# A streaming-encoder layer on one core: the opening stage loads, squares, scales and turns x's first tiles two to three slots later

## The reference

```python
h = rmsnorm(x, ln_gain)                       # x is 2048 tokens x 2048
proj = h @ w_in                               # queries, keys, values, gates, conv inputs
o_a = swa_sink_attention(q_a, k_a, v_a, ...)  # sliding window, sinks, relative bias
o_c = short_gated_conv(b_c, c_c, x_c, conv_w)
mem_h = rmsnorm(mem, mem_ln_gain)             # mem is 256 tokens x 2048
o_m = memory_cross_attention(q_m, mem_h, w_mem_kv, ...)
x = x + concat(silu(g_a) * o_a, silu(g_c) * o_c, silu(g_m) * o_m) @ w_out
```

## Time and profile before

| | us |
|---|---|
| median of three runs | 2578.4 (2577.44 to 2578.68) |
| the profiled execution | 2577.82 |
| its span | 2575.9 |
| PE busy in the span | 2561.8 (99%) |
| DVE, ACT, POOL busy | 1774.2, 1265.2, 1712.6 |
| the opening stage on PE | from 9.46 to 71.61 |

### The profile page before, as it was taken

How to read it: one execution, slowest core, us unless ns; L and a number is a source line. 1 busy time by engine, 2 the same in 40 slices (tenths; PEclk the granted TensorE clock), 3 DMA queues, 4 the chain that set the end, 5 groups by cost and what they waited for, 6 DMA issues and landing times.

```text
span 2575.9 us, 33864 instructions
## 1 busy us (share of the span) xinstructions
PE 2561.8 (99%) x11846; PEld 2112.8 (82%) x11846; DVE 1774.2 (69%) x2257; ACT 1265.2 (49%) x2629; POOL 1712.6 (66%) x1207
## 2 busy tenths in 40 slices
PE   8999999999999999999999999999999999999999
PEld 6888888888888888888888888888888888888887
DVE  6467675575746757467576767887578686887767
ACT  6454554545545555454554554544444454454443
POOL 6587667885678856787545665757567475665747
PEclk9999999999999999999999999999999999999999
DMA  7677767777667776676767443355645444334534
GB/s 252 202 253 226 245 182 242 255 232 235 192 235 262 232 236 190 231 256 226 234 191 240 146 154 101 98 163 188 197 158 169 148 139 137 96 111 139 188 111 150
DMA packets 324205, 492.26 MB, mean 191 GB/s; under 512 B 18038, under 2 KB 134852, under 8 KB 317892
## 3 DMA queue, kind: packets, MB, share of 16 engines
q1 hardware_dynamic: 209076, 296.63, 37.2%
q10 hardware_dynamic: 114960, 193.48, 21.9%
HBM read 367.61 MB, written 97.25 MB: 180 GB/s over the span
## 4 chain that ended last, share of the span: by engine, by line
PE 95%; DVE 2%; DMA 1%; ACT 1%; issue 0%; POOL 0%; SPq 0%; ACTq 0%; DVEq 0%
PE acc L1897 14%; PE acc L1899 14%; PE acc L1898 14%; PE acc L2002 7%; PE acc L2004 7%; PE acc L2006 7%; PE acc L1971 2%; PE ps_o L2006 2%; PE ps_s L2002 2%; PE ps_s L2004 2%; PE ps_s L2006 2%; PE ps_z L2002 2%; PE ps_t L2002 2%; PE ps_z L2006 2%; PE ps_o L2002 2%; PE ps_o L2004 2%
## 5 line engine op out<-in xcount | busy, mean ns | idle before, releaser
L792 POOL TENSOR_TENSOR w_both<-raw,w_both 128x512 fp32r<-128x512 f32 x889 | 1240.0, 1406 | 789.3 <-ACT w_both L918 785.2
L918 ACT ACTIVATE w_both<-raw 128x512 fp32r<-128x512 f32 x896 | 558.1, 630 | 968.5 <-PE acc L1899 335.1
L1897 PE MATMUL acc<-h_hi,w_both 128*128 128x512 f32 x768 | 311.0, 405 | 0.0
L1897 PE MATMUL acc<-w_both,h_hi 128*128 128x512 f32 x768 | 301.5, 393 | 0.0
L1899 PE MATMUL acc<-h_hi,w_both 128*128 128x512 f32 x768 | 299.6, 390 | 0.0
L1898 PE MATMUL acc<-h_lo,w_both 128*128 128x512 f32 x768 | 299.4, 390 | 0.0
L1899 PE MATMUL acc<-w_both,h_lo 128*128 128x512 f32 x768 | 299.1, 389 | 0.0
L1898 PE MATMUL acc<-w_both,h_hi 128*128 128x512 f32 x768 | 299.0, 389 | 0.0
L1763 DVE TENSOR_TENSOR a_lo<-s_sum,a_hi 128x512 fp32r<-128x512 f32 x192 | 201.7, 1085 | 87.7 <-ACT a_hi L1214 86.0
L2002 PE MATMUL acc<-w_both,a_hi 128*128 128x512 f32 x448 | 174.6, 390 | 1.6 <-DVE a_lo L1763 1.6
L2006 PE MATMUL acc<-w_both,a_lo 128*128 128x512 f32 x448 | 174.3, 389 | 0.0
(11 more groups left out here) (288 smaller groups left out, 5632.3 us busy)
## 6 DMA issues: line engine op xcount, KB each, us to landing
raw<-in_w_in SPq DMA_DIRECT2D x256, 512.0 KB, 4.6
raw<-w_sums SPq DMA_DIRECT2D x128, 512.0 KB, 3.7
w_sums<-stage ACTq DMA_DIRECT2D x32, 1024.0 KB, 5.1
probs_t<-blocks_t SPq DMA_DIRECT2D x384, 64.0 KB, 2.5
raw<-in_w_out SPq DMA_DIRECT2D x48, 512.0 KB, 3.6
stage<-in_w_in ACTq DMA_DIRECT2D x32, 512.0 KB, 5.8
h_rows<-early ACTq DMA_DIRECT2D x16, 1024.0 KB, 7.4
half_rows<-ungated ACTq DMA_DIRECT2D x16, 1024.0 KB, 8.2
```

Source lines behind the costliest of these rows:

```text
L792: nc.gpsimd.tensor_tensor(w_lo[:, at, :], raw[:, slot_mod, HALF * half:HALF * half + HALF], w_hi[:, at, :].bitcast(F32), ALU.subtract).the ...
L918: nc.scalar.activation(w_hi[:, 2 * (slot_mod % 2) + half, :], raw[:, slot_mod, HALF * half:HALF * half + HALF], ACT.Copy).then_inc(hi_read ...
L1897: nc.tensor.matmul(dst, st[0], mv[0], start=first, stop=False)
```

## The change

The change touches only the opening stage. Nothing is computed differently.

- The loads of x0 to x3 are started in slots 0, 2, 3 and 5 (`FIRST_X_LOAD_AT`); before, x0's came ahead of slot 0 and the others in slots 0, 1 and 2.
- ACT's squares: mem0 and mem1 in slots 0 and 1, x0 to x3 in slots 3, 5, 6 and 8 (`FIRST_SQUARE_AT`, now from slot to tile). Before: mem0, x0, x1, x2, mem1, x3 in slots 0 to 5. The mean on DVE follows in the same slot, the root on POOL one slot later, now always behind that slot's `low`.
- DVE's scales of x0 to x3 are in slots 5, 7, 8 and 9 (`FIRST_SCALE_AT`); before, two in slots 3 and 4, and the last after the loop.
- The 16 turns follow slots 10 to 15, with 2, 3, 2, 3, 3, 3 of them; before, slots 7 to 15 with 1, 2, 2, 2, 2, 1, 2, 2, 2.
- The semaphore counts are by tile, since the tiles now go in order.

```diff
-FIRST_TURNS = [[]] * 7 + [[0], [1, 2], [3, 4], [5, 6], [7, 8], [9], [10, 11], [12, 13], [14, 15]]
+FIRST_TURNS = [[]] * 10 + [[0, 1], [2, 3, 4], [5, 6], [7, 8, 9], [10, 11, 12], [13, 14, 15]]
-FIRST_SQUARE_AT = (0, 2, 3, 4, 1, 5)
+FIRST_SQUARE_AT = {0: 0, 1: 1, 3: 2, 5: 3, 6: 4, 8: 5}
-FIRST_X_LOAD_AT = {0: 1, 1: 2, 2: 3}
+FIRST_X_LOAD_AT = {0: 0, 2: 1, 3: 2, 5: 3}
-FIRST_SCALE_AT = {3: (1,), 4: (2, 3)}
+FIRST_SCALE_AT = {5: 2, 7: 3, 8: 4, 9: 5}
...
 POOL:
             for s in range(MEM_SLOTS):
-                if s == LAST_RSQRT:
-                    first_root(s - 1)
                 low((s + 2) % 4, s + 2)
-                if 0 < s < LAST_RSQRT:
-                    first_root(s - 1)
+                if s - 1 in FIRST_SQUARE_AT:
+                    first_root(FIRST_SQUARE_AT[s - 1])
...
 DVE, after slot 7:
-            first_low(0)
+            first_scale(FIRST_SCALE_AT[SB_SLOTS])
             mem_keys = stage[:, 2:4, :].rearrange("p m c -> p (m c)")
-            key_means(mem_keys, xt[:, 0:1024], M_HEAD, 1, mem_raw, FIRST_TURNS[SB_SLOTS])
-            before_scale = FIRST_TURNS[SB_SLOTS + 1][-1] + 1
-            for k in FIRST_TURNS[SB_SLOTS + 1]:
-                first_low(k)
+            key_means(mem_keys, xt[:, 0:1024], M_HEAD, 1, mem_raw)
+            first_mean(FIRST_SQUARE_AT[SB_SLOTS])
+            first_scale(FIRST_SCALE_AT[SB_SLOTS + 1])
             key_scale(mem_keys, 8, M_HEAD, 1)
```

More of the change, by code:

```diff
@@ L100 @@
     LAST_SLOT[_s - 1] = (_j, _b)
-FIRST_TURNS = [[]] * 7 + [[0], [1, 2], [3, 4], [5, 6], [7, 8], [9], [10, 11], [12, 13], [14, 15]]
+FIRST_TURNS = [[]] * 10 + [[0, 1], [2, 3, 4], [5, 6], [7, 8, 9], [10, 11, 12], [13, 14, 15]]
+FIRST_TURN_AT = 10
 K_TURN_MEM = 12
-FIRST_SQUARE_AT = (0, 2, 3, 4, 1, 5)
-MEM_SQUARED = 5
-FIRST_X_LOAD_AT = {0: 1, 1: 2, 2: 3}
+FIRST_SQUARE_AT = {0: 0, 1: 1, 3: 2, 5: 3, 6: 4, 8: 5}
+MEM_SQUARED = 2
+FIRST_X_LOAD_AT = {0: 0, 2: 1, 3: 2, 5: 3}
 BIAS_OUT_AT = 5
@@ L122 @@
 DVE_LOWS = (0, 3, 4, 5, 6, 7, 8)
-LAST_RSQRT = 2 + TT
 BIAS_AT = 3
@@ L825, in t_sum, with first_root @@
                     nc.gpsimd.tensor_tensor(b21, b21, b22, ALU.subtract).then_inc(t_step, 1)
-            def first_root(at):
-                tile = FIRST_SQUARE_AT[at]
+            def first_root(tile):
                 rsqrt((mem_scale if tile < 2 else x_scale)[:, tile:tile + 1], x_mean[:, tile:tile + 1], 1,
-                      x_meaned, at + 1, x_rstd)
+                      x_meaned, tile + 1, x_rstd)
             def x_item(tile):
@@ L935, in first_x_load, with first_square @@
                 act.dma_start(first_rows(2 + tile), rows_in(x, tile)).then_inc(first_in[tile], 16)
-            def first_square(at):
-                tile = FIRST_SQUARE_AT[at]
+            def first_square(tile):
                 if tile < 2:
@@ L944, in first_square @@
                     act.wait_ge(first_in[tile - 2], 16)
-                act.wait_ge(x_squares, at)
+                act.wait_ge(x_squares, tile)
                 nc.scalar.activation(squares[:, :].rearrange("p (k c) -> p k c", c=P),
@@ L1154, in _ @@
             high(1, 1, True)
-            first_x_load(0)
             mem_high(2)
@@ L1176, in _ @@
                     first_x_load(FIRST_X_LOAD_AT[s])
-                if s < len(FIRST_SQUARE_AT):
-                    first_square(s)
+                if s in FIRST_SQUARE_AT:
+                    first_square(FIRST_SQUARE_AT[s])
                 if s == BIAS_AT:
@@ L1182, in _ @@
                                          ACT.Copy).then_inc(bias_sb, 1)
-                if s == FIRST_TURNS.index([0]):
+                if s == FIRST_TURN_AT:
                     act.wait_ge(vecs_ready, 2)
@@ L1361, in _, with first_mean, first_scale @@
             dve.wait_ge(c_dve, 3)
-            def first_mean(at):
-                tile = FIRST_SQUARE_AT[at]
-                dve.wait_ge(x_squares, at + 1)
+            def first_mean(tile):
+                dve.wait_ge(x_squares, tile + 1)
                 nc.vector.tensor_scalar(x_mean[:, tile:tile + 1], x_sq[:, tile:tile + 1], 1.0 / D, EPS,
                                         ALU.mult, ALU.add).then_inc(x_meaned, 1)
-            def first_scale(at):
-                tile = FIRST_SQUARE_AT[at]
-                dve.wait_ge(x_rstd, at + 1)
+            def first_scale(tile):
+                dve.wait_ge(x_rstd, tile + 1)
                 rows = first_rows(tile)
@@ L1689, in _ @@
                 mem_low(quad)
-            for s in range(LAST_RSQRT):
+            for s in range(SB_SLOTS):
                 if s + 2 in DVE_LOWS:
@@ L1695, in _ @@
                     mem_low(quad)
[L1696 to L1703, removed]
+                if s in FIRST_SCALE_AT:
+                    first_scale(FIRST_SCALE_AT[s])
+                if s in FIRST_SQUARE_AT:
+                    first_mean(FIRST_SQUARE_AT[s])
             dve.wait_ge(vecs_ready, 2)
@@ L1714, in mem_raw @@
                     dve.wait_ge(bank_free[m], 1)
-            first_low(0)
+            first_scale(FIRST_SCALE_AT[SB_SLOTS])
             mem_keys = stage[:, 2:4, :].rearrange("p m c -> p (m c)")
-            key_means(mem_keys, xt[:, 0:1024], M_HEAD, 1, mem_raw, FIRST_TURNS[SB_SLOTS])
-            before_scale = FIRST_TURNS[SB_SLOTS + 1][-1] + 1
-            for k in FIRST_TURNS[SB_SLOTS + 1]:
-                first_low(k)
+            key_means(mem_keys, xt[:, 0:1024], M_HEAD, 1, mem_raw)
+            first_mean(FIRST_SQUARE_AT[SB_SLOTS])
+            first_scale(FIRST_SCALE_AT[SB_SLOTS + 1])
             key_scale(mem_keys, 8, M_HEAD, 1)
-            for k in range(before_scale, FIRST_TURNS[K_TURN_MEM][-1] + 1):
+            for k in range(FIRST_TURNS[K_TURN_MEM][-1] + 1):
                 first_low(k)
```

## The result

| us | before | changed |
|---|---|---|
| median | 2578.45 (2576.72 to 2578.69, 6 runs) | 2593.06 (2591.07 to 2593.65, 6 runs) |
| ratio, 95% interval | | 1.0058 [1.0048, 1.0068] |
| the profiled execution | 2577.82 | 2593.20 |
| its span | 2575.9 | 2591.3 |
| PE starts the first x group | 71.61 | 84.66 |

The changed kernel is slower by 14.6 us. Of the 15.4 us between the two profiled executions, 13.05 have come by the start of the first x group, and 1.6 of the rest right behind it, in a slow stretch of the clock.

The account below looks back on a forecast made before the run. PE, busy 99% of the span, was taken as the bound, so only its waits or clock count. From 2577.8 us, 19.9 lost less 4.9 gained gave 2592.8, rounded to 2592.5 us; range 2584 to 2599.

Parts of the forecast that it names:

- Part 1: Slots 3 to 7: later x loads end the waits for POOL's `low` and the slow clock; 4.9 us gained.
- Part 2: Before turn 0: x3's scale comes late through a chain over ACT, POOL and DVE, 18.3 us; PE stands about 9.
- Part 3: After slots 11, 13, 14 and 15: the third turn waits for its bank; 1.4 us each, 2.5 after slot 15.
- Part 4: Slow clock behind the wait before turn 0, 2.0 us, and behind slot 15, 1.85 us; none behind 1.4 us waits.
- The chain hidden: Before turn 0: x3's scale stands before slot 10's end, so its chain costs nothing; +3.7, 2581.5 us; 12%.
- the other side: Slots 3 to 7: the weights are freed and no wait follows; -4.9 us, 2573 us; 5%.
- The clock fell behind no third turn: Third turns: a rival had the clock fall behind each, three slow stretches of 1.85 us; +5.5, 2598 us; 15%.
- The weights were earlier: Up to slot 7: a rival had x1 and x2 still crowd the weights; +4.9, 2597.5 us; 8%.

Follow-up runs that it names:

- the second profile: Each kernel, before and changed, profiled once more with nothing altered; 2578.18 us before, 2592.91 us changed.
- the loads alone put back: The changed kernel with only the x loads back at their early places, squares, scales and turns left late; 2594.05 us, ratio to before 1.0057.
- the table of turns alone: The kernel before with only the changed kernel's table of turns, loads, squares and scales as before; 2587.41 us, ratio to before 1.0031.
- the four banks: The changed kernel with the turns of x in four PSUM banks instead of two; 2584.89 us, ratio to before 1.0025.
- the filled waits: The changed kernel with 60 unused identity transposes on PE ahead of turn 0 and 18 ahead of turn 15; 2589.74 us, ratio to before 1.0051.
- the chain cut: The changed kernel with x3's mean and scale ahead of DVE's keys' product and x3's root ahead of POOL's keys' root; 2584.67 us.
- the version with both: The changed kernel with x3's root and scale moved ahead of the keys' work, and four banks for the turns; 2576.76 us, ratio to before 0.9996.
- the last version: The changed kernel with four banks, x loads in slots 0, 1, 3, 4, x3's square in slot 7, its scale between keys' product and sum; 2575.07 us.

## Why the prediction was right

The forecast of 2592.5 us and the median of 2593.06 agree, and so do most of its terms. That they agree to 0.6 us is in part luck: some terms below were off and cancel. One by one:

| step | predicted | measured |
|---|---|---|
| slot 7 ends | 36.2 | 36.01 |
| end of slot 7 to turn 0 | 18.3 | 18.16 |
| wait before turn 0 | about 9 | 7.88 |
| third turns after slots 11, 13, 14 | 1.4 each | 1.30 each (wait) |
| after slot 15 | 2.5 | 2.40 (wait) |
| slow clock behind turn 0 | 2.0 | 1.8 (2.1 in the second profile) |
| slow clock behind slot 15 | 1.85 | 1.6 (1.8 in the second profile) |
| first x group starts | 84.7 (36.2 + 48.5) | 84.66 |

- **Part 1.** Right in its place and size: the waits for POOL in slots 3 to 6 are gone and the slow slot 6 with them. Wrong in its reason, in part. I gave the whole 4.9 us to the weights' earlier landing. With the loads alone put back 2.4 us are lost in the profiled pair, 1.0 by the medians and none by the ratios. The rest lies with the squares, the scales and the clock, which falls in some executions behind such a wait and not in others. That the sum came out was luck here: the squares and scales had no term of their own, and their share was booked under the loads.
- **Part 2.** The order that the prediction wrote out is the one in the timelines, link by link. Three links were off and nearly cancel. The roots of x took 0.54 and 0.55 us, with what follows them 0.6 each, not 1.0: 0.8 us less. The keys' product took 2.30 us and not 1.8: 0.5 us more. ACT's part and the start of POOL took 2.0, not 1.8. Both scales were slow, as chosen: 2.25 and 2.28 us beside POOL's `low`s, against 1.28 at 36.40, when POOL was idle. POOL is slowed as well: its pairs took 2.54 and 2.48 us while DVE stood idle, and 3.52 beside the scale and the product. The Trainium skill (GPSIMD Engine Reference, Specifications) names contention between these two engines, for instructions in a two-port mode or with two inputs; by it product and scales are all slow beside a `low`, and the trace agrees. In the kernel with the table of turns alone the product took 1.23 us: it began 0.42 us ahead of the `low`, at 43.24, and one that begins later did not slow it there.
- **The wait.** 7.88 us, where the text said about 9. Turn 0's time was right; PE was ready later. Slot 8 waited 1.01 us for the copy (0.6 in the prediction), and slot 10 waited 0.54 us for a `low`. The prediction said that the `low`s of slot 10 "cost nothing". They took 3.52 us beside DVE's product and not 2.5, and did hold PE; it changed nothing, because PE then stood still all the same.
- **Part 3.** Right: the prediction's 6.7 us are time until the next slot, and the four banks gave 6.7 us of the stage back, for 6.3 us of waits. The table of turns alone shows the same waits from the other side.
- **Part 4.** Right in size by the filled waits: 1.8 and 1.6 us for the slow stretches, and none behind a wait of 1.30. But that the clock falls behind slot 15 was not as sure as the sum took it: with the chain cut, the same 2.40 us wait had no slow stretch behind it.
- **The rivals.** The chain hidden and the other side fell with the 7.88 us wait. The clock fell behind no third turn of 1.30 us, in three of them, in each of the executions that had them. The weights were earlier: slot 7 ended at 36.01.

The sum by the measured parts: the chain with its clock 8.4, the third turns with theirs 8.2, less what the version with both leaves, 1.7 us under before (2578.45 less 2576.76; the ratio there gives 1.0, with an interval that holds 0). 8.4 + 8.2 - 1.7 = 14.9, against 14.6 measured. This is the check of 16.6 against 16.3 over again, from the side of the kernel before, and no second witness.

What stays open: how the 3.1 us of part 1 divide between the squares, the scales and the clock. And the version with both edits has a stage 2.4 us shorter than before in the profiles, while its ratio tells of 1.0 us, with an interval from 3.4 less to 1.3 more; whether its first slot (5.18 us against 3.88) always takes the difference was not tried.

## What to carry to other kernels

When work is moved to a later place to make room for a transfer, write down the lists of all engines between its new place and the first one that needs it, and add them up as one chain: here a tile scaled three slots later was tied to a chain of ten steps over three engines, 18 us long, where PE had three slots, 8 us, of work. The number of buffers sets how many items may stand in one slot: with two banks the third turn waited 1.3 us, and 2.4 us in the last slot, and with four not at all. And a transfer that crowds others is only worth what the last wait on it costs: DMA times fell from 8.5 to 5.8 us, and at most 2.4 us came of it.

## What the runs showed of the hardware

**The first slot's pace.** In nine of the twelve executions some of slot 0's first matmuls run 0.43 us apart, as in the slow stretches, and not 0.23. How long this lasts differs. In the first profiles of both kernels and in that of the table of turns alone there is, behind the first matmul's 0.56 us, at most one gap of 0.31 us. In the last version all twelve of slot 0 were slow:

```profile
9.94 0.77 PE L1888 MATMUL acc<-w_both,mix_hi 128*128 128x512 f32 x1 [0.59 <-POOL w_both L793]
10.51 0.63 PE L1889 MATMUL acc<-w_both,mix_hi 128*128 128x512 f32 x1
...
14.77 0.63 PE L1890 MATMUL acc<-w_both,mix_lo 128*128 128x512 f32 x1
...
16.44 0.47 PE L1888 MATMUL acc<-w_both,mix_hi 128*128 128x512 f32 x1
```

```profile
9.50:16.40 6.90, 6.46 (x19) 5.22 (x20) 1.38 (x5) 1.26 (x3) 2.51 (x2) 1.00 1.04 370
```

The granted clock reads 1.00 all the while; the matmuls' durations, 0.63 us, tell of the lower level. Slot 0 to slot 1 was 3.88 us in the kernel before and 4.14 in its second profile, 3.88 and 4.42 in the changed one, and 3.98, 4.37, 4.53, 4.95, 4.96, 5.18, 5.42 and 6.50 in the others. That is a spread of 2.6 us. The three executions with x's loads and squares as before are all at 4.14 or under and the nine others at 3.88 to 6.50, so part of it may hang on the change; the runs don't settle it. The Trainium skill (TensorE: Matmul & The Clock Gate, Seeing it yourself) warns that the clock's records are not to be trusted alone, and this trace agrees: the spacing of the matmuls is the better witness.

**The fall of the clock is not set by the wait's length alone.** It fell behind waits of 1.88, 2.24, 2.30 and, in four executions, 2.40 us. It did not behind 2.06, 2.33 and, in the kernel with only the chain freed, 2.40 us. It never did behind 1.30. So a wait of 2 us or so has to be priced with both ends, with and without some 1.8 us behind it (1.6 to 2.1 where it was read above).

**A tiny root has no one price.** POOL's 128x1 root took 0.54 to 0.56 us right behind a pair of `low`s (once 1.53), 0.92 to 0.95 us behind most of its waits, and 1.00 us, or 1.8 in some places, right behind a single `low`, with no wait recorded. Not every root fits: in the last version one took 0.55 us behind a wait of 1.23. The prediction took 1.0 us for roots that stood behind pairs, from the row of 0.94. Why they differ was not tried.
